# Latent norms placed among the state-space output products, and up-projections beside the output's DRAM transfer

## The chip, the cores and the metric

The kernel runs on one core of one Trainium2 chip. The metric is the device time of one execution in microseconds (us). The kernel before takes 2528.74 us, the median of three runs (2527.84 to 2532.51).

## The reference, cut to what matters

Two transformer-like blocks run on one sequence of 1024 positions and 1024 features, all in float32. The change lies in the first block, whose two branches are a state-space branch (S5) and a latent attention branch (MLA):

```python
z = x @ w_in
xs, gs, cq, ckv, kr, gm = split(z)       # 512, 512, 256, 128, 64, 512 columns
y = scan over time of (xs) -> C h        # state-space output, 512 features
y = gelu(y + d_skip * xs)
ys = y * sigmoid(y @ w_glu + b_glu) * silu(gs)
q  = (rms_norm(cq, q_norm_g) @ w_uq)     # 4 heads of 128 + 64; the 64 are rotated
kv = (rms_norm(ckv, kv_norm_g) @ w_ukv)  # 4 heads of 128 keys + 128 values
k  = concat(k_nope, rotary(kr))
ym = causal_attention(q, k, v) * silu(gm)
mix = concat(ys, ym) @ w_out
```

`rms_norm(x, g) = x * rsqrt(mean(x * x) + 1e-6) * g`, over the 128 features of the key-value latent or the 256 of the query latent.

## The kernel before

Activations lie with features on the 128 partitions and the 1024 positions along the free dimension. SBUF is cut into 50 pages of 1024 float32 columns; pages 0 to 3 are a ring of weight blocks that SyncE (SP) loads in order, each when PE has given back the block four before it. Each engine runs its own list of instructions in the order in which it is written, and semaphores join the lists. There is no planner.

PSUM has eight banks of 512 columns. `two(b)` is a pair of banks, one tile of 128 x 1024. The helper `tile` (L1641, its matmuls are L1652) makes one such tile from `kts` k-steps, each two matmuls of 512 columns; a float32 matmul stands in the trace as two records, so the tile of one k-step has four.

Around the change the stages are these, with their lines:

- Products 24 to 31, PE L1763 to L1773. Each fills one of banks 5 and 6 with the state-space output of four groups: four times a matmul 128x128 (L1770) and two with 64 rows (L1772). ACT copies each bank to `UU` (L1107 to L1112, pages 28 to 31) and counts `ssm_ps_read`; a product waits until the one two before it has been read.
- The output's trip, POOL L944 to L949. When all 32 products have been read, POOL issues eight transfers of `UU` to a DRAM tensor (L946), waits for them, and issues one transfer back into `YF` in another order (L949). Then come the mask (L952) and four transfers that copy the rotary key latent to two pages (L956, L957).
- The latent norms. `norm_act`, `norm_dve` and `norm_pe` (L728, L753, L685) make them, first of the key-value latent `CKV` (one page), then of the query latent `CQ` (two). ACT squares a page (L737), PE sums it over partitions (`sum_tiles`, L675, four matmuls with 32 output rows each), ACT takes the root (L739), DVE the reciprocal (L762), PE spreads it to all partitions (`spread_tiles`, L682), DVE multiplies (L765), ACT applies the gain (L746). PE calls them at L1775 to L1780, after the last product.
- The up-projections, PE L1782 to L1818: four key-value tiles into banks 0 to 3, eight value matmuls (L1794), four query tiles, and the query's rotary part as two pairs of tiles, both in banks 0 to 3. ACT copies the first three kinds out (L1122, L1125, L1128); DVE reads the rotary pairs (L1483 to L1492) and counts `qr_free`. ACT waits for `yf_landed` (L1119) before the first copy. The query copies go to pages 28 to 31, where `UU` lies.
- The gate product, PE L1820 to L1831, four tiles of `YF` after ACT's Gelu (L1131), with ACT's sigmoid (L1136) and DVE's products (L1495 to L1501) behind it, and then the attention of the first block (L1834).

## Time and profile before

| | us |
|---|---|
| median of three runs | 2528.74 |
| lowest, highest | 2527.84, 2532.51 |
| the profiled execution | 2508.37 |
| its span, first to last instruction | 2506.6 |
| PE busy in matmuls | 2302.1 (92%) |
| DVE, ACT, POOL busy | 894.0, 567.1, 996.7 |

The mean granted clock of TensorE is 0.955 of full speed. Times in the rows below are microseconds from the start of the span. Engines are PE (TensorE), DVE (VectorE), ACT (ScalarE), POOL (GpSimd), SP (SyncE). L12 is line 12 of the kernel, and can be the line of a helper. The idle time in brackets behind a row is that of the engine just before it, with what ended it.

### The profile page before, as it was taken

The numbers are of one execution on the slowest core, as the hardware profiler recorded it, in microseconds if no ns is written. First come the engines' busy times: TensorE is split into PE (matmuls) and PEld (weight loads), VectorE is DVE, ScalarE is ACT, GpSimd is POOL, SyncE is SP. The second block draws the span as 40 slices with busy tenths as digits, with TensorE's granted clock in tenths as the row PEclk, the third lists the DMA queues.
The fourth block names the chain that finished last, engine by engine and source line by source line (L and its number), as shares of the span: only waits on it lengthen the run. The fifth ranks groups of instructions, "written<-read, shape, count | busy, mean of one in ns | idle before, by whom it ended". The sixth has DMA issues, their size and how long they took to land.

```text
span 2506.6 us, 27327 instructions
## 1 busy us (share of the span) xinstructions
PE 2302.1 (92%) x11158; PEld 1682.6 (67%) x11158; DVE 894.0 (36%) x1257; ACT 567.1 (23%) x833; POOL 996.7 (40%) x658
## 2 busy tenths in 40 slices
PE   5999978898998499999998999997999999989995
PEld 1454443575876188557866888775888888868884
DVE  5940822442055501450046111145322333232334
ACT  3111122232011600561046000113111111111213
POOL 1533210203788057335655344332433344334441
PEclk8999978999999699999999999998999999999997
DMA  2326230001222122101211111122111111121111
GB/s 113 109 61 109 84 85 26 17 1 42 101 71 94 75 81 84 41 24 34 84 20 54 51 51 42 59 101 101 44 49 50 50 45 47 50 109 42 51 34 67
DMA packets 52439, 153.89 MB, mean 61 GB/s; under 512 B 13991, under 2 KB 16343, under 8 KB 52287
## 3 DMA queue, kind: packets, MB, share of 16 engines
q1 hardware_dynamic: 42720, 118.13, 14.2%
q10 hardware_dynamic: 6544, 23.87, 2.5%
q0 software_dynamic: 3072, 10.43, 2.2%
q8 instruction: 75, 1.23, 0.2%
q14 instruction: 28, 0.23, 0.0%
HBM read 133.37 MB, written 16.81 MB: 60 GB/s over the span
## 4 chain that ended last, share of the span: by engine, by line
PE 88%; DVE 5%; ACT 4%; DMA 2%; issue 1%; POOL 0%; ACTq 0%; DVEq 0%; SPq 0%; POOLq 0%
PE ps L1694 44%; PE ps L1652 12%; PE ps L2033 10%; PE ps L1932 4%; PE ps L1974 3%; PE ps L265 2%; PE ps L431 1%; PE ps L419 1%; PE ps L288 1%; PE ps L1772 1%; PE ps L556 1%; PE ps L568 1%; PE ps L545 1%; PE ps L413 1%; ACT back L748 1%
## 5 line engine op out<-in xcount | busy, mean ns | idle before, releaser
L1694 PE MATMUL ps<-h_high,w_parts 128*128 128x512 f32 x2688 | 732.5, 392 | 23.6 <-DVE h_low L1541 17.5
L1694 PEld LDWEIGHTS ps<-h_high,w_parts 128*128 128x128 f32 x2688 | 505.1, 189 | 129.6 <-issue 25.6
L980 POOL TENSOR_TENSOR w_parts<-front,sb_zero 128x1024 fp32r<-128x1024 f32 x138 | 267.1, 1936 | 791.1 <-PE ps L1694 467.5
L1694 PE MATMUL ps<-h_low,w_parts 128*128 128x512 f32 x1344 | 416.4, 391 | 0.0
L983 POOL TENSOR_TENSOR w_parts<-front,w_parts 128x1024 fp32r<-128x1024 f32 x138 | 349.9, 2536 | 10.9
L1694 PEld LDWEIGHTS ps<-h_low,w_parts 128*128 128x128 f32 x1344 | 253.9, 189 | 53.5
L2033 PE MATMUL ps<-ffn_parts,w_parts 128*128 128x512 f32 x1056 | 242.3, 392 | 10.7 <-DVE ffn_parts L1628 9.2
L2033 PEld LDWEIGHTS ps<-ffn_parts,w_parts 128*128 128x128 f32 x1056 | 199.8, 189 | 53.2 <-issue 11.5
L1652 PE MATMUL ps<-front 128*128 128x512 f32 x512 | 229.3, 606 | 6.1 <-DMA front<-w_in 3.4
L912 POOL TENSOR_TENSOR front<-front,sb_csilu 128x1024 f32<-128x1024 f32 x48 | 98.2, 2046 | 213.9 <-DMA front<-w_ada 198.6
L1652 PEld LDWEIGHTS ps<-front 128*128 128x128 f32 x512 | 97.7, 194 | 124.6 <-issue 119.9
L1603 DVE SCALAR_TENSOR_TENSOR back<-ps,sb_vec,back 128x1023 f32<-128x1023 f32 x44 | 56.4, 1283 | 303.4 <-ACT back L1251 303.4
L1288 DVE TENSOR_TENSOR back<-back 128x1024 f32<-128x1024 f32 (+11 forms) x62 | 94.1, 1517 | 141.5 <-ACT back L1096 68.6
L1251 ACT ACTIVATE back<-ps,sb_vec 128x1024 f32<-128x1024 f32 x44 | 53.1, 1206 | 336.8 <-PE ps L1694 336.8
L1628 DVE TENSOR_TENSOR ffn_parts<-back,ffn_parts 128x1024 fp32r<-128x1024 f32 x44 | 68.4, 1557 | 155.9 <-ACT ffn_parts L1269 155.7
L1652 PE MATMUL ps<-back,front 128*128 128x512 f32 x208 | 103.9, 661 | 21.1 <-DVEq L1489 8.0
L916 POOL TENSOR_TENSOR front<-front 128x512 f32<-128x512 f32 x96 | 120.2, 1252 | 7.5
L1652 PEld LDWEIGHTS ps<-back,front 128*128 128x128 f32 x208 | 43.5, 213 | 80.6 <-issue 68.4
L1269 ACT ACTIVATE ffn_parts<-back 128x1024 fp32r<-128x1024 f32 x44 | 46.6, 1060 | 184.9 <-PE ps L2033 183.5
L1578 DVE TENSOR_TENSOR back<-back,ps 128x1024 f32<-128x1024 f32 x8 | 9.8, 1221 | 212.2 <-PE ps L1974 212.2
L520 POOL TENSOR_SCALAR back<-back,sb_na_inv 128x512 f32<-128x512 f32 x64 | 43.5, 693 | 82.0 <-DVE sb_na_inv L486 82.0
L1932 PE MATMUL ps<-h_high,w_parts 128*128 128x512 f32 x256 | 70.5, 396 | 5.4 <-ACT back L1182 4.2
(258 smaller groups left out, 2768.8 us busy)
## 6 DMA issues: line engine op xcount, KB each, us to landing
front<-w_ada SPq DMA_DIRECT2D x48, 512.0 KB, 3.5
front<-w_up SPq DMA_DIRECT2D x44, 512.0 KB, 3.4
front<-w_down SPq DMA_DIRECT2D x22, 512.0 KB, 3.4
front<-w_in SPq DMA_DIRECT2D x16, 512.0 KB, 3.5
front<-w_out SPq DMA_DIRECT2D x16, 512.0 KB, 3.6
residual<-back ACTq DMA_DIRECT2D x2, 4096.0 KB, 12.7
front<-w_gates SPq DMA_DIRECT2D x16, 512.0 KB, 3.4
front<-xT ACTq DMA_DIRECT2D x4, 1024.0 KB, 13.2
```

Of the source, the lines that this page charges most:

```text
L912: pool.tensor_tensor(rows, rows, csilu[:].unsqueeze(2).to_broadcast((P, FT, P)), ALU.mult)\
L916: pool.tensor_tensor(x[:, 0:w], x[:, 0:w], x[:, w:2 * w], ALU.add).then_inc(S("ada_step"), 1)
L980: pool.tensor_tensor(parts[n % 2], raw, zero[:, 0:1].to_broadcast((P, PAGE)), ALU.add)\
L983: pool.tensor_tensor(parts[2 + n % 2], raw, parts[n % 2].bitcast(F32), ALU.subtract).then_inc(S("w_split"), 1)
L1288: link(dve.tensor_tensor(o, a, b, op))
L1603: dve.scalar_tensor_tensor(y[:, 1:], src[:, :SEQ - 1], one(conv, n + (half * N_UP)), y[:, 1:], ALU.mult, ALU.add).then_inc(S("up_left"), 1)
L1628: dve.tensor_tensor(AR[2 + kk % 2], ACTV[:, kk % N_UP, :], AR[kk % 2].bitcast(F32), ALU.subtract).then_inc(S("ffn_split"), 1)
L1652: mm = pe.matmul(ps[:, bank + nt, :], ring[:, slot, at + k * step:at + k * step + P], rhs(k0 + k)[:, nt * BANK:(nt + 1) * BANK], start=sta ...
L1694: mm = pe.matmul(ps[:, bank + nt, :], w_[:, k * P:(k + 1) * P], x_[k][:, nt * BANK:(nt + 1) * BANK], start=at == 0 and n == 0, stop=at == ...
L1932: mm = pe.matmul(ps[:, 2 * j + nt, :], WR[n % 2 + w_][:, at:at + P], x_[2 * b + k][:, nt * BANK:(nt + 1) * BANK], start=b == 0 and k == 0 ...
L1974: mm = pe.matmul(ps[:, 4 + k // 4 * 2 + nt, :], WR[n % 2 + w_][:, k * P:(k + 1) * P], x_[k][:, nt * BANK:(nt + 1) * BANK], start=k % 4 == ...
L2033: mm = pe.matmul(ps[:, 2 * m + nt, :], WR[n % 2 + w_][:, at:at + P], AR[kk % 2 + x_][:, nt * BANK:(nt + 1) * BANK], start=k == 0 and q == ...
```

## The change

The norms of the two latents get functions of their own and are placed between the products: sums in bank 7, spread values in the first halves of banks 0 to 3. PE, ACT and DVE call them at the places given by `x == 25`, `26` and `28`. The temporary pages move, since the products still read page 44 up to its middle. On POOL the rotary key transfers and the mask go ahead of the output's trip. On ACT the wait for the transfer back moves behind the query copies, and a wait for the output in DRAM stands ahead of them. The second rotary pair uses banks 4 to 7, so PE waits for DVE once less, and DVE waits for the last product before it writes the rotated keys (page 44).

```diff
--- before.py
+++ after.py
@@ -765,8 +765,55 @@
                 dve.tensor_tensor(quarters(dst(k)), quarters(src(k)), SPREAD, ALU.mult).then_inc(S("norm_scaled"), 1)
 
 
+
+        LATENT = ps[:, 0:4, 0:256]
+
+        def latent(i):
+
+            return (CKV, "kv_norm", V("kv_norm_g", 0)) if i == 0 else (CQ[:, i - 1, :], "q_norm", V("q_norm_g", i - 1))
+
+        def latent_sums_pe(pe, i):
+            pe.wait_ge(S("norm_square"), tiles_to("kv_norm", i + 1))
+            ones_ = ones_q if i else ones_kv
+            sum_tiles(pe, 7, ones_[:], TEMPS_2[i % 2], i < 2, i != 1).then_inc(S("norm_square_used"), 1)
+
+        def latent_spread_pe(pe, N):
+            pe.wait_ge(S("norm_rstd"), norms_to(N))
+            if N == "q_norm":
+                pe.wait_ge(S("norm_scaled"), tiles_to("kv_norm", 1))
+            else:
+                pe.wait_ge(S("z_free"), 16)
+            for j in range(4):
+                at = slice(32 * j, 32 * j + 32)
+                mm = pe.matmul(ps[:, j, 0:256], pick[at, :], TEMPS_2[2][at, 256:512], start=True, stop=True)
+            mm.then_inc(S("norm_spread"), 1)
+
+        def latent_square_act(act, i):
+            if i == 2:
+                act.wait_ge(S("norm_square_used"), tiles_to("kv_norm", 1))
+            act.activation(TEMPS_2[i % 2], latent(i)[0], ACT.Square).then_inc(S("norm_square"), 1)
+
+        def latent_root_act(act, N, i):
+            act.wait_ge(S("norm_square_used"), tiles_to("kv_norm", i + 1))
+            if N == "q_norm":
+                act.wait_ge(S("norm_spread"), norms_to("kv_norm"))
+            act.activation(TEMPS_2[2][:, 256:512], ps[:, 7, 0:256], ACT.Sqrt, bias=eps[:, 1:2]).then_inc(S("norm_std"), 1)
+
+        def latent_gain_act(act, i):
+            x, _, gain = latent(i)
+            act.wait_ge(S("norm_scaled"), tiles_to("kv_norm", i + 1))
+            act.activation(x, x, ACT.Copy, scale=gain).then_inc(S("norm_ready"), 1)
+
+        def latent_dve(dve, N, tiles):
+            dve.wait_ge(S("norm_std"), norms_to(N))
+            dve.reciprocal(TEMPS_2[2][:, 256:512], TEMPS_2[2][:, 256:512]).then_inc(S("norm_rstd"), 1)
+            dve.wait_ge(S("norm_spread"), norms_to(N))
+            for i in tiles:
+                x = quarters(latent(i)[0])
+                dve.tensor_tensor(x, x, LATENT, ALU.mult).then_inc(S("norm_scaled"), 1)
+
         TEMPS_1 = (page(24), page(25), page(26))
-        TEMPS_2 = (page(44), page(45), page(46))
+        TEMPS_2 = (page(45), page(46), cols(44 * PAGE + 512, 45 * PAGE))
         TEMPS_3 = (page(12), page(13), page(14))
 
         BLOCKS_WIN = 32
@@ -941,6 +988,13 @@
             pool.dma_start(page(47).bitcast(I32), t["pos"].partition_broadcast(P)).then_inc(S("pos_landed"), 16)
 
             ada_sum(15)
+            pool.wait_ge(S("norm_ready"), tiles_to("q_norm", 2))
+            for half in range(2):
+                pool.dma_start(page(46)[64 * half:64 * half + 64, :], KR[0:64, :]).then_inc(S("kr_landed"), 16)
+                pool.dma_start(page(47)[64 * half:64 * half + 64, :], KR[64:128, :]).then_inc(S("kr_landed"), 16)
+            pool.wait_ge(S("dve_step"), DVE_STEP["cm_zero"])
+            pool.dma_start(CM[:, SEQ - P:SEQ], t["causal"]).then_inc(S("cm_landed"), 16)
+
             pool.wait_ge(S("ssm_ps_read"), 32)
             for s in range(STEP):
                 pool.dma_start(y_dram.rearrange("(g c) t -> c g t", c=GC)[:, :, s * CHUNKS:(s + 1) * CHUNKS],
@@ -948,13 +1002,6 @@
             pool.wait_ge(S("y_in_dram"), 16 * STEP)
             pool.dma_start(YF, y_dram.rearrange("(k p) t -> p k t", p=P)).then_inc(S("yf_landed"), 16)
 
-            pool.wait_ge(S("dve_step"), DVE_STEP["cm_zero"])
-            pool.dma_start(CM[:, SEQ - P:SEQ], t["causal"]).then_inc(S("cm_landed"), 16)
-
-            pool.wait_ge(S("norm_ready"), tiles_to("q_norm", 2))
-            for half in range(2):
-                pool.dma_start(page(46)[64 * half:64 * half + 64, :], KR[0:64, :]).then_inc(S("kr_landed"), 16)
-                pool.dma_start(page(47)[64 * half:64 * half + 64, :], KR[64:128, :]).then_inc(S("kr_landed"), 16)
             pool.memset(zero[:], 0.0).then_inc(S("pool_step"), 1)
             pool.wait_ge(S("pool_step"), POOL_STEP["zero"])
             pool.wait_ge(S("glu_used"), 4)
@@ -1104,29 +1151,36 @@
             act.activation(SIN, COS, ACT.Sin).then_inc(S("act_step"), 1)
             act.activation(page(47), COS, ACT.Sin, scale=0.5).then_inc(S("act_step"), 1)
 
+            latent_square_act(act, 0)
+            latent_square_act(act, 1)
             for x in range(24, 32):
                 r, odd = (x - 24) // 2, x % 2
                 act.wait_ge(S("ssm_ps"), x + 1)
                 act.activation(UU[:, 8 * r + odd:8 * r + 8:2, :],
                                ps[:, 5 + x % 2, :].rearrange("p (g n) -> p g n", g=4), ACT.Copy)\
                     .then_inc(S("ssm_ps_read"), 1)
-
-            norm_act(act, "kv_norm", 1, lambda k: CKV, lambda k: CKV, lambda k: V("kv_norm_g", 0), None,
-                     1, False, TEMPS_2)
-            norm_act(act, "q_norm", 2, lambda k: CQ[:, k, :], lambda k: CQ[:, k, :],
-                     lambda k: V("q_norm_g", k), None, 1, False, TEMPS_2)
-
-            act.wait_ge(S("yf_landed"), 16)
+                if x == 25:
+                    latent_root_act(act, "kv_norm", 0)
+                    latent_square_act(act, 2)
+                if x == 26:
+                    latent_gain_act(act, 0)
+                    latent_root_act(act, "q_norm", 2)
+                if x == 28:
+                    latent_gain_act(act, 1)
+                    latent_gain_act(act, 2)
+
             for m in range(4):
                 act.wait_ge(S("kv_tile"), m + 1)
                 act.activation(KN[:, m, :], two(2 * (m % 2)), ACT.Copy).then_inc(S("kv_free"), 1)
             for kt in range(8):
                 act.wait_ge(S("kv_tile"), 4 + kt + 1)
                 act.activation(VT[:, kt, :], ps[:, kt % 4, :], ACT.Copy).then_inc(S("kv_free"), 1)
+            act.wait_ge(S("y_in_dram"), 16 * STEP)
             for m in range(4):
                 act.wait_ge(S("q_tile"), m + 1)
                 act.activation(QN[:, m, :], two(2 * (m % 2)), ACT.Copy).then_inc(S("q_free"), 1)
 
+            act.wait_ge(S("yf_landed"), 16)
             for k in range(4):
                 act.activation(YF[:, k, :], YF[:, k, :], ACT.Gelu_apprx_tanh).then_inc(S("yg_ready"), 1)
             for m in range(4):
@@ -1468,8 +1522,8 @@
             link(dve.tensor_scalar(SIN, SIN, rope_c[:, 1:2], None, ALU.mult))
             tt(COS, page(47), page(47), ALU.mult)
             link(dve.tensor_scalar(COS, COS, -2.0, 1.0, ALU.mult, ALU.add))
-            norm_dve(dve, "kv_norm", 1, lambda k: CKV, lambda k: CKV, False, TEMPS_2)
-            norm_dve(dve, "q_norm", 2, lambda k: CQ[:, k, :], lambda k: CQ[:, k, :], False, TEMPS_2)
+            latent_dve(dve, "kv_norm", (0,))
+            latent_dve(dve, "q_norm", (1, 2))
             dve.wait_ge(S("norm_ready"), tiles_to("q_norm", 2))
 
             link(dve.memset(CM, 0.0))
@@ -1477,6 +1531,7 @@
             link(dve.memset(QR, 0.0))
 
             dve.wait_ge(S("kr_landed"), 64)
+            dve.wait_ge(S("ssm_ps"), 32)
             tt(KROT, page(46), COS, ALU.mult)
             tt(page(46), page(47), SIN, ALU.mult)
             tt(KROT, KROT, page(46), ALU.add)
@@ -1484,8 +1539,8 @@
                 dve.wait_ge(S("qr_tile"), m + 1)
                 for i in range(2):
                     h = slice(64 * i, 64 * i + 64)
-                    tt(QR[h, 2 * m + i, :], two(0)[h, :], COS[h, :], ALU.mult)
-                tt(page(46), two(2), SIN, ALU.mult)
+                    tt(QR[h, 2 * m + i, :], two(4 * m)[h, :], COS[h, :], ALU.mult)
+                tt(page(46), two(4 * m + 2), SIN, ALU.mult)
                 dve.sem_inc(S("qr_free"), 1)
                 for i in range(2):
                     h = slice(64 * i, 64 * i + 64)
@@ -1771,14 +1826,16 @@
                     for i in range(2):
                         mm = pe.matmul(o, CP[h, i, q, GC:GC + P], SS[h, i, q, :], start=False, stop=i == 1)
                 mm.then_inc(S("ssm_ps"), 1)
-
-            pe.wait_ge(S("z_free"), 16)
-            pe.wait_ge(S("ada_read"), 1)
-            pe.wait_ge(S("ssm_ps_read"), 32)
-            norm_pe(pe, "kv_norm", 1, None, ones_kv[:], False, TEMPS_2)
-            pe.wait_ge(S("norm_scaled"), tiles_to("kv_norm", 1))
-            norm_pe(pe, "q_norm", 2, None, ones_q[:], False, TEMPS_2)
-
+                if x == 25:
+                    latent_sums_pe(pe, 0)
+                if x == 26:
+                    latent_spread_pe(pe, "kv_norm")
+                    latent_sums_pe(pe, 1)
+                    latent_sums_pe(pe, 2)
+                if x == 28:
+                    latent_spread_pe(pe, "q_norm")
+
+            pe.wait_ge(S("norm_scaled"), tiles_to("q_norm", 2))
             pe.wait_ge(S("norm_ready"), tiles_to("kv_norm", 1))
             b = B_UKV
             block_landed(B_UKV)
@@ -1810,15 +1867,16 @@
             pe.wait_ge(S("q_free"), 4)
             for m in range(2):
                 if m == 1:
-                    pe.wait_ge(S("qr_free"), 1)
-                tile(0, (B_UQ + 1) % RING, lambda k: CQ[:, k, :], kts=2, at=m * P, step=BANK)
-                tile(2, (B_UQ + 1) % RING, lambda k: CQ[:, k, :], kts=2, at=(2 + m) * P, step=BANK)\
+                    pe.wait_ge(S("ada_read"), 1)
+                    pe.wait_ge(S("ssm_ps_read"), 32)
+                tile(4 * m, (B_UQ + 1) % RING, lambda k: CQ[:, k, :], kts=2, at=m * P, step=BANK)
+                tile(4 * m + 2, (B_UQ + 1) % RING, lambda k: CQ[:, k, :], kts=2, at=(2 + m) * P, step=BANK)\
                     .then_inc(S("qr_tile"), 1)
             pe.wait_ge(S("qr_tile"), 2)
             pe.sem_inc(S("w_used"), 1)
 
             pe.wait_ge(S("yg_ready"), 4)
-            pe.wait_ge(S("qr_free"), 2)
+            pe.wait_ge(S("qr_free"), 1)
             for m in range(4):
                 block_landed(B_GLU + m // 2)
                 if m >= 2:
```

## Rows read from the trace of the kernel before

**Rows 1.** The page's chain that ended last, its line by engine.
```profile
PE 88%; DVE 5%; ACT 4%; DMA 2%; issue 1%; POOL 0%; ACTq 0%; DVEq 0%; SPq 0%; POOLq 0%
```

**Rows 2.** The chain in order of time, 338 to 365: start us, us, what.
```profile
338.20 4.41 POOL ssm_out_by_feature L946 x7
342.61 11.35 DMA ssm_out_by_feature<-back
354.25 10.15 DMA back<-ssm_out_by_feature
```

**Rows 3.** PE's timeline: start us, us, engine, line, operation, tiles, count [idle before, releaser].
```profile
336.56 0.71 PE L1772 MATMUL ps<-back 64*128 64x128 f32 x4
339.00 0.64 PE L675 MATMUL ps<-back,sb_ones_kv 128*32 128x256 f32 x8 [1.72 <-ACT back L737]
342.55 1.24 PE L682 MATMUL ps<-back,sb_pick 32*128 32x256 f32 x8 [2.92 <-DVE back L762]
347.35 1.94 PE L675 MATMUL ps<-back,sb_ones_q 128*32 128x256 f32 x16 [3.56 <-ACT back L737]
351.67 1.23 PE L682 MATMUL ps<-back,sb_pick 32*128 32x256 f32 x8 [2.38 <-DVE back L762]
352.83 6.12 PE L1652 MATMUL ps<-back,front 128*128 128x512 f32 x8
365.50 6.61 PE L1652 MATMUL ps<-back,front 128*128 128x512 f32 x8 [6.55 <-ACT back L1122]
373.22 7.13 PE L1794 MATMUL ps<-front,back 128*128 128x512 f32 x16 [1.11 <-ACT back L1122]
381.09 13.97 PE L1652 MATMUL ps<-back,front 128*128 128x512 f32 x32 [0.73 <-ACT back L1125]
396.26 7.11 PE L1652 MATMUL ps<-back,front 128*128 128x512 f32 x16 [1.21 <-ACT back L1128]
407.33 9.61 PE L1652 MATMUL ps<-back,front 128*128 128x512 f32 x16 [3.96 <-DVEq L1489]
420.94 16.48 PE L1652 MATMUL ps<-back,front 128*128 128x512 f32 x32 [4.00 <-DVEq L1489]
437.73 13.97 PE L1652 MATMUL ps<-back,front 128*128 128x512 f32 x32 [0.30 <-PE ps L1652]
```

**Rows 4.** Windows: length, busy time (count) of each engine, granted clock, DMA share, GB/s.
```profile
304.00:338.00 34.00, 33.27 (x190) 25.57 (x189) 3.49 (x5) 6.87 (x12) 0.00 (x0) 1.00 0.09 32
338.00:370.00 32.00, 15.60 (x54) 5.95 (x55) 12.58 (x8) 11.02 (x12) 8.56 (x15) 0.59 0.69 166
395.00:398.00 3.00, 1.79 (x5) 0.87 (x5) 0.00 (x0) 2.88 (x3) 0.00 (x0) 1.00 0.48 175
404.00:407.00 3.00, 0.00 (x0) 0.00 (x0) 2.93 (x3) 0.00 (x0) 0.00 (x0) 0.75 0.00 0
```

**Rows 5.** ACT's timeline.
```profile
337.31 0.60 ACT L1110 ACTIVATE back<-ps 128x512 f32<-128x512 f32 x1 [3.63 <-PE ps L1772]
...
338.87 1.28 ACT L739 ACT_TABLE_LOAD   x1
340.16 0.47 ACT L739 ACTIVATE back<-ps,sb_eps 128x256 f32<-128x256 f32 x1
...
397.43 3.89 ACT L1131 ACTIVATE back<-back 128x1024 f32<-128x1024 f32 x4
```

**Rows 6.** DVE's timeline.
```profile
340.74 1.75 DVE L762 RECIPROCAL back<-back 128x256 f32<-128x256 f32 x1 [31.02 <-ACT back L739]
343.86 1.22 DVE L765 TENSOR_TENSOR back<-back,ps 128x1024 f32<-128x1024 f32 x1 [1.36 <-PE ps L682]
...
403.48 3.74 DVE L1288 TENSOR_TENSOR back<-ps,back 64x1024 f32<-64x1024 f32 x3 [30.85 <-PE ps L1652]
```

**Rows 7.** POOL's key transfers: an issue in its timeline, and four to landing.
```profile
358.60 0.54 POOL L956 DMA_DIRECT2D back<-back  x1
...
back<-back POOLq DMA_DIRECT2D x4, 256.0 KB, 7.1
```

## The prediction

> **What bounds the kernel now.** I read the page's chain first. TensorE (PE) carries 88% of it [rows 1], so a microsecond taken off PE's path is a microsecond off the end, and the question is where that path is not matmul. The chain in order of time answers it for the stretch of the change [rows 2]: when the last state-space output product has been read, the end hangs on GpSimd (POOL) issuing eight transfers at 338.20, on their landing until 353.96, and on the transfer back until 364.40. For 27 us no engine's arithmetic is on the chain.
>
> PE's timeline shows what PE did meanwhile and after [rows 3]. The last product ends at 337.27. Then four small groups of norm matmuls with waits between them, two key-value tiles at 352.83, a wait of 6.55 us, two more tiles, the value tiles, the query tiles, two rotary pairs with waits of 3.96 and 4.00 us, and the gate product's two halves, ending at 451.70. The stretch is 451.70 - 337.27 = 114.4 us. The windows show its second cost [rows 4]: the granted clock, 1.00 in the products, averages 0.59 between 338 and 370, which is mostly the lower level (1.2 GHz), and falls again in the wait at 404. Sixteen records of 128x512 take 7.11 us at the full clock, while the sixteen at 352.83 and 365.50 took 12.73 us [rows 3].
>
> **What changes, part by part.** All of it lies before or inside this stretch.
>
> (a) The latent norms go between the products. Three groups of sums and two spreads leave the stretch and land inside the products. In the products PE is the bound: ScalarE (ACT) reads one in 0.60 us after 3.63 us idle [rows 5], so a product is 4.23 us. What must fit is the norms' chain through the other engines. Square 0 and 1 (passes over a page; four such passes of the Gelu take 3.89 us, so about 1 us each [rows 5]) come just before the first read, which has a spare bank and 3.63 us of slack. The products start at 303.4 (337.27 less eight of 4.23); product 25 ends at 311.9, its sums take 0.64 [rows 3], and ACT reads product 25 until 312.6, loads the Sqrt table (1.28) and takes the root (0.47) [rows 5] until 314.4; VectorE's (DVE) reciprocal, 1.75 [rows 6], ends at 316.2. PE is then in product 26 until 316.8, so the spread waits for nothing. The third square follows the root, at 315.5, before PE asks for it. DVE's scaling is 1.22 [rows 6], the gain again one pass; the query root's chain (0.47 + 1.75) has products 27 and 28, 8.4 us. The last two scalings and gains have three products. Nothing should stall. PE itself pays for the added instructions: sums 3 x 0.64 = 1.9 [rows 3]. A spread was 1.24 at the lower clock [rows 3, 4]; the full clock can at best halve it, so its bounds are 0.6 and 1.24; I take 0.8, since part of so short a group is not clocked. Two are 1.6. With 0.2 for hand-overs (a) costs 3.7 us, bounds 3.0 and 5.1 (all groups at the times of the lower clock: 0.64 + 1.94 + 2 x 1.24).
>
> ACT's table load stands directly before the root in the trace, and the root starts 0.01 us after its end [rows 5]. The Trainium skill (ScalarE: Activation LUTs, What ACT_TABLE_LOAD costs) adds a drain of 1.38 us to every switch. By that the first spread would wait some 0.8 us, and (a) would be 4.5; the sum here goes by the row.
>
> (b) Up-projections run beside the transfer. Their loops and sizes are unchanged, so PE's work is, at the full clock: key-value 7.1, values 7.1, queries 14.0, two rotary pairs 14.2, gate product 28.0 [rows 3], together 70.4. Between them stay the short pauses that are buffer hand-overs: 1.1 before the values, 0.7 before the queries, 1.2 before the rotary pair, 0.3 in the gate product [rows 3], and some 0.3 at the start: 3.6 us. The wait of 6.55 goes because ACT no longer waits for the transfer back before its key-value copies.
>
> (c) The second rotary pair gets banks 4 to 7, so both waits of 4 us for DVE go. DVE's first three products (3.74 us [rows 6]) run beside the second pair (7.1 us), and the gate product needs only the first pair's banks. DVE's second turn, the same products and two additions, runs beside the gate product.
>
> (d) ACT's waits move. Its query copies now wait for the output to be in DRAM. The products end at 337.27 + 3.7 = 341.0, so the eight issues begin at about 342.0; at 15.8 us from first issue to last landing [rows 2] they are in at 357.8. The first query tile is ready for its copy at about 360.8, and PE wants the bank at 364.3, so the spare is 5 us. The transfer back (10.2 [rows 2]) lands at 368.2; ACT ends its query copies at about 372.3, then needs 1.28 + 3.89 for table and Gelu [rows 5], so the gate product's input is ready at 377.5 and PE asks at 386. Behind ACT's wait are only these copies and the Gelu, behind those PE's queries and gate product: spare 5 and 8 us.
>
> (e) POOL's queue. It now waits for the norms (about 331.5) and for DVE's mask memset (about 333.5), issues four key transfers of 0.54 [rows 7] and the mask, and then waits for the last product. It is free at about 336, 6 us before it is needed. In the trace the key transfers land in a median of 7.1 us beside the transfer back [rows 7]; here they have the queue to themselves until 342. DVE waits for them, then for product 32, before rotating the keys; it is otherwise idle until 379. SyncE's queue loads by PE's give-backs, which all move with PE.
>
> **The sum.** The stretch becomes 3.7 + 70.4 + 3.6 = 77.7 us, against 114.4: 36.7 us less. By parts: 11.9 from the norms, 6.5 from the wait, 8 from the two rotary waits, the rest almost all the clock (5.6 in the key-value tiles, about 5 in the second rotary pair and the gate product). Everything after is chained to PE through hand-overs inside the kernel and moves along. Against the profiled execution, 2508.37 us (span 2506.6), that is 2471.7. The median of the runs shown is 20.4 us above this execution, and I do not know where these 20 us lie, so I carry the difference over: 2528.7 - 36.7 = 2492.0.
>
> **Rivals.** *The clock falls in the new stretch, and the result is slower.* If each hand-over pause (0.7 to 1.2 us) or the small matmuls let the clock drop, the 70.4 us of (b) double: 77.7 + 70.4 = 148.1, against 114.4, or 33.7 slower, 2562. It becomes slower than before once more than 36.7 of the 70.4 us run at 1.2 GHz; a few of them cost one for one. Against it: between 395 and 398 PE paused 1.21 us and the windows there show 1.00; only the pause of nearly 4 us at 403 brought 0.75, and 9.61 us for the group behind it [rows 3, 4]. The new stretch has no pause above 1.2. The Trainium skill (TensorE: Matmul & The Clock Gate, A second HAM failure mode) says that micro-idles between groups of matmuls can make the clock swing; by that rule this rival would hold at least in part. The trace disagrees for pauses of this size. For mostly half clock 3%.
>
> *The output's trip becomes the bound.* The eight transfers may queue behind key transfers still under way, or run slower beside weight loads and PE's traffic. Up to 5 us it costs nothing, beyond that one for one at the query copies. If all four key transfers had to land one after the other first (4 x 7.1 from 334), the output would start at 362 instead of 342, 15 us past the spare: the gain would be 22, 2507. For it speaks only that POOL's queue now has them in front; against it the 6 us of slack. 8%.
>
> *The norms don't fit between the products*, that is, the change doesn't do what it says: PE, in order, waits inside the products for root, reciprocal and scaling. In the trace these waits are 1.72 + 2.92 + 3.56 + 2.38 = 10.6 us [rows 3]. If all stayed, the gain is 26, 2503. 8%.
>
> *Something outside the stretch takes it back*, wholly or mostly: nothing in the trace is timed from before 338 except the loads, which are far ahead. The result would be 2528 or so; 3%.
>
> **How the numbers follow.** Forecast 2492, chance 78%. Its own bounds: (a) 3.0 to 5.1; the pauses, 3.6 by up to 3 either way; the phase of the clock at the next stage, 2 us; the runs shown spread over 4.7 us; and the unplaced 20 us, some of which may be transfer time that the change hides too, which reaches further down, or matmul time, which does not. That gives 2481 to 2500. The range goes up to 2508 to take in the norms and the trip, and leaves out the slow clock. What a measurement of this kernel can tell from no change is 0.2%, 5 us. Faster by more: 94%; within: 3%; slower: 3%.
>
> **What would show it.** In the profile after: products 24 to 31 with 3 to 5 us more between first start and last end and no PE wait above 1 us among them; no 6.5 us wait at the key-value tiles; clock 1.00 from 304 to the end of the gate product; the sixteen-record groups at 7.1; the gate product ending near 415; ACT's query copies released by PE. Wrong would be: a PE wait for DVE or ACT at the spreads; a query copy released by a DMA; a clock of 0.5 anywhere before the attention; or a stretch of 78 us with a span that is not 37 shorter.

## The result, and the profile after

The changed kernel takes 2469.35 us (median of four executions, 2467.11 to 2472.43) against 2528.34 us before (four, 2527.84 to 2532.51): ratio 0.9764, 95% interval 0.9747 to 0.9781, 59.0 us less where 36.7 were forecast. The profiled executions are closer together: 2467.11 us against 2508.37, that is 41.3 less. In some executions of either kernel TensorE's clock falls to 1.2 GHz about 3 us after product 24 begins, which costs about 25 us (the experiments show it); by their times all four executions behind the median of before were of this kind, while the profiled one was not, and none of the four after was.

The chain after, by engine, answers to [rows 1]. DMA's share falls from 2% to 1%, since the output's trip [rows 2] is no longer on the chain. PE's two points less are not read as the change's: most of them lie in the group L1749 (L1694 before), outside the stretch, which carries 41.8% of the chain for 43.6%, while POOL's share grows.

```profile
PE 86%; DVE 4%; ACT 4%; POOL 2%; DMA 1%; issue 1%; ACTq 0%; DVEq 0%; POOLq 0%; SPq 0%
```

PE's timeline of the changed kernel, with the rows that answer to [rows 3] (columns as there):

```profile
309.79 0.64 PE L675 MATMUL ps<-back,sb_ones_kv 128*32 128x256 f32 x8
...
314.58 0.71 PE L788 MATMUL ps<-back,sb_pick 32*128 32x256 f32 x8
315.23 1.07 PE L675 MATMUL ps<-back,sb_ones_q 128*32 128x256 f32 x16
...
324.68 0.71 PE L788 MATMUL ps<-back,sb_pick 32*128 32x256 f32 x8
...
337.37 0.71 PE L1827 MATMUL ps<-back 64*128 64x128 f32 x4
338.01 7.13 PE L1707 MATMUL ps<-back,front 128*128 128x512 f32 x16
346.25 7.13 PE L1851 MATMUL ps<-front,back 128*128 128x512 f32 x16 [1.11 <-ACT back L1174]
354.12 13.97 PE L1707 MATMUL ps<-back,front 128*128 128x512 f32 x32 [0.73 <-ACT back L1177]
369.30 13.97 PE L1707 MATMUL ps<-back,front 128*128 128x512 f32 x32 [1.21 <-ACT back L1181]
383.57 13.97 PE L1707 MATMUL ps<-back,front 128*128 128x512 f32 x32 [0.30 <-PE ps L1707]
397.85 13.97 PE L1707 MATMUL ps<-back,front 128*128 128x512 f32 x32 [0.30 <-PE ps L1707]
```

The norms' small groups stand between the products with no wait before any of them. The four key-value tiles are one group of sixteen records in 7.13 us where they were 6.12 + 6.61 with 6.55 of waiting; the two rotary pairs are one group of 13.97; the gate product ends at 411.82. From the first product (301.36; before 303.42) to there it is 110.5 us, against 148.3: 37.8 less. The windows answer to [rows 4]: length, busy time of each engine, granted clock (third from the end), DMA share, GB/s.

```profile
308.00:341.00 33.00, 33.00 (x203) 23.52 (x202) 14.17 (x10) 11.64 (x15) 4.65 (x9) 1.00 0.16 37
341.00:360.00 19.00, 17.15 (x40) 7.25 (x39) 0.96 (x1) 8.92 (x13) 3.92 (x7) 1.00 0.80 188
...
400.00:415.00 15.00, 13.37 (x36) 6.06 (x34) 7.24 (x5) 2.23 (x2) 0.00 (x0) 1.00 0.14 50
```

ACT and POOL, for [rows 5] and [rows 7]: the root, the query copies and the Gelu; the mask, the output's trip and the transfer back.

```profile
311.81 0.47 ACT L800 ACTIVATE back<-ps,sb_eps 128x256 f32<-128x256 f32 x1
...
357.89 1.02 ACT L1181 ACTIVATE back<-ps 128x1024 f32<-128x1024 f32 x1 [3.87 <-PE ps L1707]
...
370.46 3.89 ACT L1185 ACTIVATE back<-back 128x1024 f32<-128x1024 f32 x4
```

```profile
331.37 0.57 POOL L996 DMA_DIRECT2D back<-causal  x1
339.00 5.02 POOL L1000 DMA_DIRECT2D ssm_out_by_feature<-back  x8 [7.05 <-ACT back L1159]
354.78 0.79 POOL L1003 DMA_DIRECT2D back<-ssm_out_by_feature  x1 [10.76 <-DMA ssm_out_by_feature<-back]
```

The query copy at 357.89 was released by PE, not by a DMA, and the eight transfers were in by 354.78. The Gelu was through at 374.35 and PE took up the gate product at 383.57.

### The profile page after: what moved, and what is told of

It reads as the page before. It is cut to its first block, busy times and chain, and to the rows that moved or that the text cites. A ratio compares the mean times of both kernels' runs of the same rounds, so it can differ in the third digit from the quotient of the medians.

```text
span 2465.3 us, 27328 instructions
## 1 busy us (share of the span) xinstructions
PE 2285.3 (93%) x11158; PEld 1676.8 (68%) x11158; DVE 893.8 (36%) x1257; ACT 567.3 (23%) x833; POOL 997.5 (40%) x658
## 3 DMA queue, kind: packets, MB, share of 16 engines
q8 instruction: 75, 1.23, 0.2%
## 4 chain that ended last, share of the span: by engine, by line
PE 86%; DVE 4%; ACT 4%; POOL 2%; DMA 1%; issue 1%; ACTq 0%; DVEq 0%; POOLq 0%; SPq 0%
PE ps L1749 42%; PE ps L1707 12%; PE ps L2091 10%; PE ps L1990 4%; PE ps L2032 4%; PE ps L265 2%; PE ps L431 1%; PE ps L419 1%; PE ps L288 1%; PE ps L1827 1%; PE ps L556 1%; PE ps L568 1%; PE ps L413 1%; ACT back L748 1%; PE ps L545 1%
## 5 line engine op out<-in xcount | busy, mean ns | idle before, releaser
L1749 PE MATMUL ps<-h_high,w_parts 128*128 128x512 f32 x2688 | 732.5, 392 | 23.6 <-DVE h_low L1596 17.5
L1749 PEld LDWEIGHTS ps<-h_high,w_parts 128*128 128x128 f32 x2688 | 505.2, 189 | 129.5 <-issue 25.7
L1749 PE MATMUL ps<-h_low,w_parts 128*128 128x512 f32 x1344 | 416.4, 391 | 0.0
L1749 PEld LDWEIGHTS ps<-h_low,w_parts 128*128 128x128 f32 x1344 | 253.9, 189 | 53.5
L1658 DVE SCALAR_TENSOR_TENSOR back<-ps,sb_vec,back 128x1023 f32<-128x1023 f32 x44 | 56.4, 1282 | 303.4 <-ACT back L1305 303.4
L1707 PE MATMUL ps<-back,front 128*128 128x512 f32 x208 | 92.7, 604 | 6.9 <-issue 4.0
## 6 DMA issues: line engine op xcount, KB each, us to landing
residual<-back ACTq DMA_DIRECT2D x2, 4096.0 KB, 12.8
```

The source lines that it names most:

```text
L1658: dve.scalar_tensor_tensor(y[:, 1:], src[:, :SEQ - 1], one(conv, n + (half * N_UP)), y[:, 1:], ALU.mult, ALU.add).then_inc(S("up_left"), 1)
L1707: mm = pe.matmul(ps[:, bank + nt, :], ring[:, slot, at + k * step:at + k * step + P], rhs(k0 + k)[:, nt * BANK:(nt + 1) * BANK], start=sta ...
L1749: mm = pe.matmul(ps[:, bank + nt, :], w_[:, k * P:(k + 1) * P], x_[k][:, nt * BANK:(nt + 1) * BANK], start=at == 0 and n == 0, stop=at == ...
```

## The experiments

Beside them the kernel before ran 98 times (12 of them as e0_before): 67 executions at 2500 to 2512 us, median 2505.3 in the first 81, and 31 at 2527 to 2534, median 2530.3, none between. The mean granted clock over the whole span splits in the same way, 0.955 to 0.963 in the lower group and 0.944 to 0.950 in the upper. Where a kernel shows such groups I compare group with group; the medians and ratios over all executions mix them.

**The kernel before, once more.** No edit.

> The kernel before, once more, with a profile beside its timed executions. Theory A (the profiled execution of before, 2508, was an odd one: most executions are 20 us longer for a reason inside the kernel, such as a lower granted clock or a transfer that lands later somewhere): timed 2528, and a profile near 2528 shows in one stretch where the 20 us are. Theory B (the profile came from another chip or session): timed and profiled agree here at one level, 2508 or 2528, with the rows of the stretch unchanged (last product to end of gate product 114.4 us).

Measured: 2507.16 us (2501.58 to 2534.09, 12 executions), ratio 0.9984 (0.9942 to 1.0027); eight below 2510, four above 2528. This time the profiled execution, span 2528.1, was one of the upper ones. PE's rows around the first product and the last, windows (columns as above), and one of ACT's eight reads of a product:

```profile
304.43 0.20 PE L1674 MATMUL ps<-sb_ones,front 128*64 128x1 f32 x1
304.96 0.46 PE L1770 MATMUL ps<-back 128*128 128x128 f32 x2 [0.34 <-PE ps L1674]
...
361.66 1.22 PE L1772 MATMUL ps<-back 64*128 64x128 f32 x4
```

```profile
304.00:308.00 4.00, 3.66 (x22) 2.66 (x22) 2.16 (x3) 2.78 (x4) 0.00 (x0) 0.95 0.58 197
308.00:312.00 4.00, 4.00 (x15) 3.10 (x14) 2.67 (x3) 0.92 (x2) 0.00 (x0) 0.50 0.18 70
...
332.00:364.00 32.00, 30.88 (x100) 23.40 (x99) 0.00 (x0) 3.47 (x6) 0.19 (x1) 0.50 0.00 1
```

```profile
317.96 0.60 ACT L1110 ACTIVATE back<-ps 128x512 f32<-128x512 f32 x1 [6.90 <-PE ps L1772]
```

Against [rows 5], where ACT idles 3.63 us between two reads, it idles 6.90: a product takes 7.50 us instead of 4.23, with PE busy all the time. The fall came about 3 us after the first product's start at 304.96, and the clock was still 0.50 when the last one ended at 362.88: 57.9 us for 33.85. Eight products would give 8 x 3.27 = 26.2 us; part of the first one still ran at the full clock, which leaves 24.1, and the groups differ by 25.0. Theory A holds in its reason, a lower granted clock in one stretch, and not in its count: only a third of the executions are the long ones, and the timed median is near 2507.

**The changed kernel, twice more.** No edit.

> The changed kernel, once more. Theory A (the change also takes away what makes before's usual executions 20 us longer): ratio 0.976 again, 59 us. Theory B (the medians of before and after are not of the same chip): the ratio is 0.985, 37 to 41 us.

> The changed kernel once more, for the share of executions whose products run at 1.2 GHz. Theory (the change does not touch what lets the clock fall; before has it in 27 of 81): about a third, one to four of these executions near 2495, the rest near 2469. Rival (the norms between the products keep the clock up, and the measured 59 us are all the change's): none or one near 2495.

Measured: 2485.58 us (2468.40 to 2498.16, six), ratio 0.9868 (0.9802 to 0.9933), and 2474.44 (2465.86 to 2500.57, six), ratio 0.987 (0.9826 to 0.9914). With the first four that is 16 executions: nine at 2465.9 to 2472.4, five at 2493.1 to 2500.6 and two at 2478. The clock falls here too, in 7 of 16 against 35 of 102 in the kernel before (its first four included): the change does not prevent it, and the theory of the second holds. Theory B of the first is near in its number and wrong in its reason: each set of timings of before has both levels in it, so another chip is not needed. At the full clock the six of the first ten give 2469.4 against 2505.3, ratio 0.986 (0.985 to 0.987 by resampling), 35.9 us; all nine give 2468.4, 36.9 us. The two at 2478 are new. The profile of e0_after shows one:

```profile
308.00:312.00 4.00, 4.00 (x15) 3.10 (x15) 1.78 (x2) 1.44 (x2) 0.00 (x0) 0.50 0.02 6
...
320.00:324.00 4.00, 4.00 (x14) 3.10 (x15) 0.58 (x1) 0.00 (x0) 0.00 (x0) 0.50 0.00 0
324.00:328.00 4.00, 4.00 (x31) 1.95 (x30) 1.22 (x1) 1.30 (x2) 0.00 (x0) 0.59 0.00 0
328.00:332.00 4.00, 4.00 (x25) 3.15 (x24) 1.75 (x1) 0.92 (x3) 0.00 (x0) 1.00 0.01 4
```

The clock comes back at about 327, when PE has come through the spread (324.74) and most of the sixteen records of sums behind product 26. In the profiles of norms_only, pool_old and after_again it stayed at 0.50 behind the same instructions, so that these bring it back is not shown.

**Norms alone, and order alone.** norms_only is the changed kernel with the old order on POOL, the old wait on ACT and one set of banks:

```diff
-            pool.wait_ge(S("norm_ready"), tiles_to("q_norm", 2))
...
             pool.wait_ge(S("ssm_ps_read"), 32)
...
+            pool.wait_ge(S("norm_ready"), tiles_to("q_norm", 2))
...
+            act.wait_ge(S("yf_landed"), 16)
             for m in range(4):
                 act.wait_ge(S("kv_tile"), m + 1)
...
-            act.wait_ge(S("y_in_dram"), 16 * STEP)
...
+                    pe.wait_ge(S("qr_free"), 1)
```

> The norms between the products, everything else as before: ACT waits for the transfer back before the key-value copies, one set of banks for both rotary pairs, key transfers after the output's trip. Theory (the trip sets the end as long as ACT waits for it first): the products take 2.8 us more, the trip starts 2.8 us later, and the kernel is 3 us slower than before (2531 against 2528). Rival (each part is worth its own term): 11.9 us faster.

Measured: eight at 2504.2 to 2510.0, median 2508.7, and four at 2534 to 2536.4: 3.5 and 5.1 us slower than before's groups (over all, ratio 1.0006, 0.9964 to 1.0048). The place of the norms by itself is worth less than nothing. PE has its tiles ready early and stands:

```profile
366.36 5.90 PE L1706 MATMUL ps<-back,front 128*128 128x512 f32 x8
395.26 5.11 PE L1706 MATMUL ps<-back,front 128*128 128x512 f32 x8 [23.00 <-ACT back L1175]
```

order_only is the kernel before with ACT's two waits moved and banks 4 to 7 for the second rotary pair.

```diff
-            act.wait_ge(S("yf_landed"), 16)
             for m in range(4):
                 act.wait_ge(S("kv_tile"), m + 1)
...
+            act.wait_ge(S("y_in_dram"), 16 * STEP)
...
+            act.wait_ge(S("yf_landed"), 16)
...
-                tile(0, (B_UQ + 1) % RING, lambda k: CQ[:, k, :], kts=2, at=m * P, step=BANK)
+                tile(4 * m, (B_UQ + 1) % RING, lambda k: CQ[:, k, :], kts=2, at=m * P, step=BANK)
```

> The norms behind the products as before; ACT's waits moved and banks 4 to 7 for the second rotary pair, as after. Theory: the key-value tiles start at 352.8 at the lower clock and run on without a wait, the gate product ends near 429 instead of 451.7: 23 us faster than before. Rival (the norms' place carries most of it): under 15 us faster. If the extra 20 us of the timed executions go with either part, that part shows 20 us more than this.

Measured: three at 2479.4 to 2489.1 and nine at 2505.9 to 2509.9 (ratio over all 0.9951, 0.9911 to 0.9991). The groups lie 21.6 and 21.8 below before's, where the theory had 23; the first of these rests on three executions that spread over 10 us. In the profile it is 125.3 us from the first product to the end of the gate product, 23.0 less than the 148.3 of before. That nine of twelve fell is more than elsewhere, though nothing is edited ahead of the products; in yf_first below it was two of twelve. Why, no run shows. The key-value tiles run without a wait behind the norms, at first at the lower clock:

```profile
347.21 1.23 PE L682 MATMUL ps<-back,sb_pick 32*128 32x256 f32 x8 [2.38 <-DVE back L762]
348.37 9.24 PE L1653 MATMUL ps<-back,front 128*128 128x512 f32 x16
358.73 7.13 PE L1795 MATMUL ps<-front,back 128*128 128x512 f32 x16 [1.11 <-ACT back L1121]
```

Alone the parts give +3.5 and -21.7, together -36 (POOL's order, which neither has, is worth nothing: pool_old below): the norms' place pays once nothing behind them waits for the trip.

**One set of banks.** The changed kernel with both pairs in one set, on PE and DVE.

```diff
...
-                    pe.wait_ge(S("ada_read"), 1)
-                    pe.wait_ge(S("ssm_ps_read"), 32)
-                tile(4 * m, (B_UQ + 1) % RING, lambda k: CQ[:, k, :], kts=2, at=m * P, step=BANK)
+                    pe.wait_ge(S("qr_free"), 1)
+                tile(0, (B_UQ + 1) % RING, lambda k: CQ[:, k, :], kts=2, at=m * P, step=BANK)
...
-            pe.wait_ge(S("qr_free"), 1)
+            pe.wait_ge(S("qr_free"), 2)
```

> The changed kernel with both rotary pairs in banks 0 to 3 and both waits for DVE back. Theory: the two waits of 4.0 us and the clock behind them (2.5 us each) return, 12 to 13 us slower than the changed kernel at the same clock in the products: 2482 where that is 2469, 2508 where it is 2495. Rival (the Gelu or DVE would have been waited for anyway): under 5 us.

Measured: five at 2479.5 to 2482.9, one at 2511.5 (ratio 0.9894, 0.983 to 0.9958); 12.8 us above the changed kernel's 2469.4. Both waits and the lower clock behind each are back:

```profile
380.95 9.71 PE L1707 MATMUL ps<-back,front 128*128 128x512 f32 x16 [3.96 <-DVEq L1544]
394.66 16.53 PE L1707 MATMUL ps<-back,front 128*128 128x512 f32 x32 [4.00 <-DVEq L1544]
```

**ACT's wait.** The changed kernel with ACT's waits as before.

```diff
+            act.wait_ge(S("yf_landed"), 16)
             for m in range(4):
                 act.wait_ge(S("kv_tile"), m + 1)
...
-            act.wait_ge(S("y_in_dram"), 16 * STEP)
...
-            act.wait_ge(S("yf_landed"), 16)
```

> The changed kernel with ACT waiting for the transfer back before its key-value copies, as before; the second rotary pair keeps its own banks. Theory (the other up-projections run beside the trip only because of this wait's new place): the third key-value tile waits until about 366 in place of 342 and starts at the lower clock, 25 to 28 us slower than the changed kernel, 2496 (or 2522 where the products run at 1.2 GHz). Rival (the norms' place carries the gain): under 12 us slower.

Measured: ten at 2489.6 to 2495.8, median 2493.2, two at 2517 and 2522 (ratio 0.9945, 0.9907 to 0.9983): 23.8 us slower than the changed kernel, 1 us short of the theory's 25.

```profile
339.25 3.70 PE L1706 MATMUL ps<-back,front 128*128 128x512 f32 x8
365.65 5.36 PE L1706 MATMUL ps<-back,front 128*128 128x512 f32 x8 [22.70 <-ACT back L1175]
```

The wait is 22.70 us, and the group behind it lost another 1.7 to the clock.

**POOL's order.** The changed kernel with mask and key transfers behind the trip.

```diff
-            pool.wait_ge(S("norm_ready"), tiles_to("q_norm", 2))
...
             pool.dma_start(YF, y_dram.rearrange("(k p) t -> p k t", p=P)).then_inc(S("yf_landed"), 16)
+            pool.wait_ge(S("dve_step"), DVE_STEP["cm_zero"])
...
+            pool.wait_ge(S("norm_ready"), tiles_to("q_norm", 2))
```

> The changed kernel with the mask and the four key transfers after the output's trip on POOL's queue, as before. Theory: the rotated keys are late by 30 us but DVE needs them by 376 only, so the time does not move by more than 1 us: 2469 (2495). Rival (the keys land beside the transfer back at 370 to 376 and DVE's first rotary products wait): up to 8 us slower.

Measured: three at 2466.0 to 2471.2, three at 2493.3 to 2498.4 (ratio 0.9876, 0.9816 to 0.9936): no difference in either group. In its profile, one of the upper group, DVE gets the keys at 399.42 and still idles 4.00 us before PE's first pair:

```profile
399.42 3.75 DVE L1342 TENSOR_TENSOR back<-back 128x1024 f32<-128x1024 f32 x3 [46.23 <-DMA back<-back]
407.16 3.74 DVE L1342 TENSOR_TENSOR back<-ps,back 64x1024 f32<-64x1024 f32 x3 [4.00 <-PE ps L1707]
```

**What lets the clock fall.** Five kernels were aimed at this. pause is the kernel before with a wait for ACT's last sine ahead of the products:

```diff
+            pe.wait_ge(S("act_step"), ACT_STEP["rope_sin"])
             pe.wait_ge(S("dve_step"), DVE_STEP["states_ready"])
```

> The kernel before, with PE held for 3.9 us ahead of the products (it waits for ACT's last sine). Theory (the products only keep the clock level at which they begin): the pause brings the clock to 0.50, all eight products run at 7.5 us instead of 4.2, and every execution is at about 2535 (2505 + 3.5 + 26), none at 2509. Rival (the fall is drawn anew for each execution somewhere in the products): two groups as in before, near 2509 and 2534. Second rival (the clock comes back inside the products): about 2512.

Measured: 2534.39 us, all twelve at 2529.9 to 2536.5 (ratio 1.0068, 1.0033 to 1.0104). The profile has the clock at 0.50 from the first product at 302.23 to the end of the last at 362.25, and ACT's reads as far apart as in e0_before:

```profile
302.23 0.80 PE L1771 MATMUL ps<-back 128*128 128x128 f32 x2 [3.92 <-ACT back L1105]
...
317.33 0.60 ACT L1110 ACTIVATE back<-ps 128x512 f32<-128x512 f32 x1 [6.90 <-PE ps L1773]
```

no_pause takes the shortest edit the other way. `ada_last` (L1668 before) ends with a wait for its own matmuls and a hand-over to ACT; for the sums ahead of the products both move behind product 24:

```diff
+                if a == 15:
+                    return
                 pe.wait_ge(S(back), ada_given(a))
                 pe.sem_inc(S("ada_done"), 1)
...
                 mm.then_inc(S("ssm_ps"), 1)
+                if x == 24:
+                    pe.wait_ge(S("w_used"), ada_given(15))
+                    pe.sem_inc(S("ada_done"), 1)
```

> The changed kernel, with the wait and the hand-over of the ada sums (0.34 us without a matmul) moved behind product 24. Theory (the thin spell of four one-column matmuls and this pause ahead of the products is what lets the clock fall): executions near 2495 become rare or vanish, all near 2469. Rival (the products themselves are too thin and any execution can fall): two groups as in the changed kernel, 2469 and 2495, in about the same shares.

> The kernel of no_pause once more, for the share: six of six executions were near 2469. Theory: again none near 2495. Rival: two or three of six.

> The kernel before with the same one edit as no_pause: the hand-over of the ada sums and its 0.34 us moved behind product 24. Theory (that pause and the one-column matmuls beside it are what lets the clock fall at the start of the products): 12 executions near 2505, none near 2530; by the share of low ones in before so far, 21 of 58, twelve without one would come up by luck once in 200 times. Rival (each execution can fall whatever stands ahead of the products): about four of twelve near 2530.

Measured on the changed kernel: 2469.46 us (2468.02 to 2471.60, six; ratio 0.9824, 0.9771 to 0.9877) and 2468.46 (2465.44 to 2472.07, six; 0.9835, 0.979 to 0.9879). On the kernel before: 2504.99 (2500.78 to 2508.19, twelve; 0.997, 0.9939 to 1.0001). None of these 24 executions fell. PE's timeline of no_pause at the spot shows the first product directly behind the one-column matmuls; with the hand-over in place PE stood for 0.34 us between them, as in e0_before above. Behind product 24, where the hand-over now is, PE does not pause:

```profile
304.74 0.20 PE L1729 MATMUL ps<-sb_ones,front 128*64 128x1 f32 x1
304.86 0.49 PE L1827 MATMUL ps<-back 128*128 128x128 f32 x2
...
309.09 0.49 PE L1827 MATMUL ps<-back 128*128 128x128 f32 x2
```

The pair also gives the change's own worth with nothing mixed in: 2469.1 (twelve) against 2505.0 (twelve), 35.9 us.

more_pause goes the other way on the changed kernel: three more one-column matmuls, each waited for.

```diff
             ada_last(15, "w_used", "w_used")
+            for r in range(3):
+                pe.matmul(ps[:, 7, 256 + r:257 + r], ident[:], ones[:, 0:1], start=True, stop=True).then_inc(S("idle"), 1)
+                pe.wait_ge(S("idle"), r + 1)
```

> The changed kernel with three more one-column matmuls ahead of the products, each waited for (about 0.34 us each, 1 us in all). Theory (the pause ahead of the products lets the clock fall, the more often the longer it is): the share of executions near 2496 (2495 + 1) rises clearly above a third, to most of them. Rival (it is not the pause): the share stays at a third and the upper group is near 2470.

Measured: 2481.80 us (2469.88 to 2501.30, twelve; ratio 0.9906, 0.987 to 0.9941): two executions near 2470, five at 2476 to 2482, five at 2497 to 2501. By their times the clock fell in ten of twelve. The three matmuls did not make PE's pause longer, as the expectation has it: the trace counts them as busy, 1.23 us in all, and leaves 0.36 us of idle time around them where 0.34 us stood before. What grew, by 1.1 us, is the thin spell ahead of the products. The profiled execution is of the middle group: down 2 us after the products' start, up again at 326, in the product behind the sums.

```profile
298.73 1.23 PE L1816 MATMUL ps<-sb_ones,sb_ident 128*128 128x1 f32 x6 [0.18 <-PE ps L1729]
300.02 0.49 PE L1828 MATMUL ps<-back 128*128 128x128 f32 x2
```

```profile
300.00:304.00 4.00, 3.98 (x18) 3.06 (x18) 1.91 (x2) 3.90 (x4) 0.00 (x0) 0.75 0.66 252
...
320.00:324.00 4.00, 4.00 (x26) 2.35 (x28) 0.73 (x1) 0.60 (x1) 0.00 (x0) 0.50 0.00 0
324.00:328.00 4.00, 4.00 (x27) 2.48 (x19) 2.24 (x2) 1.51 (x2) 0.00 (x0) 0.76 0.02 4
328.00:332.00 4.00, 4.00 (x24) 3.15 (x24) 0.00 (x0) 0.60 (x1) 0.00 (x0) 1.00 0.00 0
```

warm adds to the changed kernel two 128x256 matmuls in each product, written into the product's bank and then overwritten:

```diff
+                    if j % 2 == 0:
+                        pe.matmul(ps[:, 5 + x % 2, j * P:(j + 2) * P], ident[:], XN[:, j, 0:256], start=True, stop=True)
```

> The changed kernel, with two further 128x256 matmuls in every product (written into the product's own bank and overwritten by it; the result is unchanged). They cost 16 x 0.44 = 7 us at the full clock. Theory (the products are too thin to bring the clock back): with them it never stays down, all executions near 2476, none above 2485. Rival (density does not matter): two groups, near 2476 and 2510.

Measured: 2474.71 us (2472.66 to 2477.37, six; ratio 0.9845, 0.9792 to 0.9898). By their times none fell, for 5.3 us more. The pause of 0.34 us is still there in this kernel, so denser products look like a second way to the same end, a dearer one; but at a share of about a third six without a fall come up by luck once in 13 times, so this is not shown.

The best of all is no_pause, the change plus the moved hand-over: no faster than the changed kernel at its best, but at 2465 to 2472 in twelve of twelve executions.

## Why the prediction was wrong

The step that failed is the last sentence of the sum: "The median of the runs shown is 20.4 us above this execution, and I do not know where these 20 us lie, so I carry the difference over: 2528.7 - 36.7 = 2492.0." The difference is not a constant that could be carried. The 20 us were the 1.2 GHz level in the products, which the four executions shown of before had and those of after had not. The sum against the profiled execution, 2471.7, needed no correction: like with like the change is worth 35.9 us for 36.7 forecast, and the other 23 us of the measured 59.0 are what the median of before's four, 2528.34, lies above the 2505.3 of its lower group. Why all four of before fell and none of the four after, when about a third do otherwise, stays open; four of four would come up by luck about once in 65 times, none of four once in six.

The prediction's own sign of being wrong, a clock of 0.5 before the attention, does stand in the profiles of e0_after and after_again, in the products and not in the new stretch. Had the four executions after been mixed like the six of e0_after, whose median is 2485.58, the time would have lain inside the stated range, and its executions at 2493 to 2501 are near the 2492 forecast; but that would have been luck, since the prediction had no reason for these 20 us.

Term by term:

(a) The norms between the products: forecast 3.7 us, bounds 3.0 to 5.1; measured 36.65 - 33.85 = 2.8, just under the lower bound. A spread was 0.65 (taken as 0.8) and the two later sum groups together 1.0 (taken as 1.3), since the last records of a group overlap with the next product. PE waited for nothing among the products. The root starts 0.02 us after the table load again, and the first spread did not wait: the drain of 1.38 us that the Trainium skill adds (ScalarE: Activation LUTs, What ACT_TABLE_LOAD costs) does not show here either.

(b), (c) Pauses and groups came out as written, 1.11, 0.73, 1.21 and 0.30 us, with all sixteen-record groups at 7.0 to 7.13; from the end that the products would have had (335.21) to the end of the gate product it is 76.6 us, for 77.7 forecast. one_pair and yf_first show these terms by taking them back: 12.8 us for the banks (forecast 13 with the clock), 23.8 for ACT's wait.

(d), (e) The trip's times came some 3 us early, 2.1 of them because the products began that much earlier, its spare was never used, and POOL's order was worth nothing by itself (pool_old), as argued.

Of the rivals, "The clock falls in the new stretch" held the right resource in the wrong place: the argument against it, that pauses up to 1.2 us leave the clock at 1.00, was read from stretches of dense matmuls [rows 3, 4] and does not hold ahead of the products, where 0.34 us can be enough. The span's other 3.5 us (41.3 less 37.8) are 2.1 before the first product and 1.4 after the gate product, which no step named. The first product starts at 298.96 to 306.27 in the profiles here of kernels that have the same instructions up to it, so the 2.1 are no more than this spread.

## What to carry to other kernels

Before costing a change, look where the profiled execution stands among the timed ones: a gap of 20 us between them is a finding to be placed, by a second profile if it can be had, and not a constant. Moving a chain of small steps into a stretch in which most of its engines idle pays only if what follows does not wait for a long transfer anyway; here the parts alone gave +3.5 and -22 us, together -36. And a queue hand-over of a third of a microsecond on TensorE, ahead of a stretch of small matmuls, was worth moving into that stretch: by the shares and the 25 us above, an estimate of 9 us in the mean of many executions, and a time that no longer jumps.

## What the runs showed of the hardware

With no norms in it, a stretch of small matmuls kept the TensorE clock that it had about 3 us after its start. Products of 128x128 and 64x128 matmuls, with PE busy throughout, ran 34 us at 1.00 (before) and 60 us at 0.50 (pause, which begins them at 0.50); where the clock fell it did so 2 to 3 us after the first product began, and in the kernel before (e0_before) it then stayed at 0.50 to the last one, 55 us.

What PE did before the fall was four one-column matmuls and a pause. With no pause between them and the products the clock fell in 0 of 24 executions; with the pause of 0.34 us in 61 of 166 (all kernels here that have it, but for warm), told by their times; with some 1.1 us of single one-column matmuls more, at nearly the same idle time, in 10 of 12; with 3.9 us idle in 12 of 12. The share with 0.34 us differs much from kernel to kernel, 2 of 12 to 9 of 12, and what decides in a single execution stays open: of the ten profiles with this pause the five with a fall begin the products at 303.3 to 306.3, the five without at 299.0 to 303.4, and no run tests whether this is more than chance.

In dense stretches of 512-column matmuls pauses of 1.1 to 1.2 us did not lower the clock in the profiles before and after. The Trainium skill (TensorE: Matmul & The Clock Gate, A second HAM failure mode) says that frequent micro-idles between groups of matmuls can make the clock swing. The trace agrees in part: the pauses between the dense groups did nothing, one pause ahead of the products can be enough, and the clock can then stay down for the whole stretch. In the changed kernel it came back during or just behind the norms' spread and sums in some executions (the two at 2478; by their times five of ten in more_pause) and not in others.
